# Weight blocks and activation planes placed modulo 256 bytes, and a down projection in three passes instead of two

## The reference, cut to what matters

```python
h = h + hybrid_mixer(rms_norm(h, g), w_in, ...)      # w_in 1024 x 3592, w_out 1024 x 1024
h = h + conv_ffn(rms_norm(h, g), w_up, ..., w_down)  # w_up 1024 x 5632, w_down 2816 x 1024
...
for l in range(2):
    h = h + 0.5 * swiglu(rmsnorm(h, ffn1_norm[l]), w_gate, w_up, w_down)   # 1024 x 2816 twice, 2816 x 1024
    h = h + hybrid_mixer_2(rmsnorm(h, mix_norm[l]), w_in, ...)             # 1024 x 4608 and three smaller
    h = h + 0.5 * swiglu(rmsnorm(h, ffn2_norm[l]), w_gate, w_up, w_down)
```

## Time and profile before

| | |
|---|---|
| median of three runs | 1459.07 us (1458.87 to 1459.16) |
| the profiled execution's own time | 1458.79 us |
| its span, first to last instruction | 1457.0 us |
| around the span | 1.8 us |
| TensorE matmuls, busy / share / count | 1449.5 us, 99%, 11473 |
| VectorE busy | 903.2 us, 62% |
| ScalarE busy | 770.0 us, 53% |
| GpSimd busy | 493.6 us, 34% |
| DMA, mean | 172 GB/s |

### The profile page before, as it was taken

The page is one execution under the profiler, slowest core; times in us unless marked ns, Lnnn a source line. Parts: engine busy times, 40 slices in busy tenths (PEclk is TensorE's granted clock), DMA queues, the critical chain, the costliest instruction groups (busy, mean ns, idle before and its releaser), DMA issues.

```text
span 1457.0 us, 30945 instructions
## 1 busy us (share of the span) xinstructions
PE 1449.5 (99%) x11473; PEld 1417.6 (97%) x11473; DVE 903.2 (62%) x1576; ACT 770.0 (53%) x1113; POOL 493.6 (34%) x213
## 2 busy tenths in 40 slices
PE   9999999999999999999999999999999999999998
PEld 8899999889999999999999999999999999999987
DVE  6438888756446469988644434444447898864533
ACT  6546555555444446567544544444444657654443
POOL 6550000534334303710333432433420570044342
PEclk9999999999999999999999999999999999999999
DMA  7435666645556445455555654655644635567763
GB/s 269 131 113 162 177 185 203 210 149 173 173 173 213 163 131 165 143 156 166 175 175 173 203 180 129 185 172 182 201 151 145 174 119 186 174 195 202 208 189 114
DMA packets 74634, 250.92 MB, mean 172 GB/s; under 512 B 15808, under 2 KB 16704, under 8 KB 74560
## 3 DMA queue, kind: packets, MB, share of 16 engines
q1 hardware_dynamic: 74272, 249.38, 55.5%
q10 hardware_dynamic: 288, 0.54, 0.1%
HBM read 247.79 MB, written 1.05 MB: 171 GB/s over the span
## 4 chain that ended last, share of the span: by engine, by line
PE 98%; DVE 1%; ACT 0%; issue 0%; DVEq 0%; ACTq 0%
PE W L1697 27%; PE W L1698 27%; PE W L1699 27%; PE W L1785 3%; PE XP L1849 2%; PE XQ L1849 2%; PE W L1784 1%; PE W L1749 1%; PE W L1800 1%; PE W L1799 1%; PE W L1750 1%; PE W L1798 1%; PE W L1751 1%; PE XQ L1962 0%; PE XP L1854 0%
## 5 line engine op out<-in xcount | busy, mean ns | idle before, releaser
L463 POOL TENSOR_TENSOR wlo<-raw,whi 128x1024 fp32r<-128x1024 f32 (+1 forms) x185 | 473.1, 2562 | 913.0 <-ACT whi L538 912.6
L1697 PE MATMUL W<-xh,whi 128*128 128x272 f32 (+2 forms) x2400 | 689.6, 287 | 0.0
L1698 PE MATMUL W<-xl,whi 128*128 128x272 f32 (+2 forms) x2400 | 687.5, 286 | 0.0
L1699 PE MATMUL W<-xh,wlo 128*128 128x272 f32 (+2 forms) x2400 | 685.8, 286 | 0.0
L538 ACT ACTIVATE whi<-raw 128x1024 fp32r<-128x1024 f32 (+1 forms) x440 | 480.6, 1098 | 109.7 <-PE W L1699 68.2
L1697 PEld LDWEIGHTS W<-xh,whi 128*128 128x128 f32 x2400 | 452.4, 189 | 2.2 <-issue 1.2
L1699 PEld LDWEIGHTS W<-xh,wlo 128*128 128x128 f32 x2400 | 452.3, 188 | 0.0
L1698 PEld LDWEIGHTS W<-xl,whi 128*128 128x128 f32 x2400 | 451.1, 188 | 0.2
L1023 DVE TENSOR_TENSOR wlo<-raw,whi 128x1024 fp32r<-128x1024 f32 (+1 forms) x255 | 331.8, 1302 | 80.3 <-ACT whi L538 80.0
L1697 PE MATMUL W<-ax,whi 128*128 128x272 f32 (+2 forms) x816 | 234.5, 287 | 0.4 <-DVE ax L1467 0.3
L1699 PE MATMUL W<-ax,wlo 128*128 128x272 f32 (+2 forms) x816 | 234.3, 287 | 0.0
(11 more groups left out here) (293 smaller groups left out, 1401.0 us busy)
## 6 DMA issues: line engine op xcount, KB each, us to landing
raw<-in_w SPq DMA_DIRECT2D x377, 512.0 KB, 3.7
raw<-in_w SPq DMA_DIRECT2D x64, 704.0 KB, 4.1
proj<-proj SPq DMA_DIRECT2D x16, 64.0 KB, 3.8
scr<-in_cst SPq DMA_DIRECT2D x1, 1000.0 KB, 8.3
h<-in_hT SPq DMA_DIRECT2D x3, 272.0 KB, 4.4
raw<-in_w SPq DMA_DIRECT2D x2, 256.0 KB, 3.8
proj<-in_gain SPq DMA_DIRECT2D x1, 512.0 KB, 5.0
out<-proj SPq DMA_DIRECT2D x4, 128.0 KB, 1.8
```

Source lines behind the costliest of these rows:

```text
L463: pool.tensor_tensor(wlo[:, j, 0:cols], raw[:, j, 0:cols], whi[:, j, 0:cols].bitcast(F32), ALU.subtract).then_inc(lo_ready[j], 1)
L1697: pe.matmul(out, whi[:, j, w], mh, start=start and k == 0, stop=False, skip_group_check=True)
L1698: pe.matmul(out, whi[:, j, w], ml, start=False, stop=False, skip_group_check=True)
L1699: ins = pe.matmul(out, wlo[:, j, w], mh, start=False, stop=stop and k == len(rhs) - 1, skip_group_check=True)
```

## The change

Four things change together.

1. **Weight blocks** are written to `whi` and `wlo` not back to back but at a place and with a step that follow the moving operand: `step` is 128 + 16 against `xh` and `xl` (whose chunks step by 272), 128 + 32 against `ax` in the products over 1024 channels, 128 in the down projections. The place is worked out so that a weight block always begins 16 elements (64 bytes) past the beginning of its moving chunk modulo 64 (26 elements where the first token is 14). Slots are 1440 wide instead of 1408. `raw` stays packed. In the last down projection the moving weights begin where the stationary activation begins modulo 64.
2. **`ax`** becomes `[P, 2, FC, ROW]` with ROW = 288, so `ah` and `al` of a chunk begin at the same place modulo 64 and chunks alternate between two places. The chunks of a down projection are dealt to its two slabs by parity (0, 2, 4... and 1, 3, 5...), so that inside a slab the place is constant.
3. **The first down projection** uses the three passes of `slab`, 256 columns each; `halves` and `residual_halves` are gone, and `residual` makes one addition where two were.
4. **Room**: `cst` keeps 256 columns, its other 688 land in a part of `proj` by a second DMA, and VectorE waits for GpSimd's copy of them (`minus_ready`) before it writes to that part. GpSimd's loops over slabs of the first projections and of the mixers are written out.

```diff
+LINE, PITCH = 64, S11 + 32
+WHI_AT, WLO_AT, X_AT, ROW = 0, 0, 0, T + 16
+Place = namedtuple("Place", "blocks width step hi lo")
+X_BEHIND = {0: -16, T_A: -26, T_B: -16}
+ACT_BEHIND = {0: (-16, -16), T_A: (-26, -26), T_B: (-16, -16)}
+DOWN_BEHIND = {0: (-16, -16), T_B: (-16, -16)}
+TOKEN_BEHIND = (0, 0)
+def column(moving, weights, j, behind):
+    return (moving - weights - LINE // 2 * (j % 2) - behind) % LINE
+def x_place(t, j):
+    return Place(DC, P, P + T % LINE, column(X_AT + t, WHI_AT, j, X_BEHIND[t]), column(X_AT + t, WLO_AT, j, X_BEHIND[t]))
...
+def d_places(t):
+    high, low = DOWN_BEHIND[t]
+    return tuple(Place(HALF, P, P, column(X_AT + t + j % 2 * ROW, WHI_AT, j, high),
+                       column(X_AT + t + j % 2 * ROW, WLO_AT, j, low)) for j in range(4))
...
-        whi = sb("whi", [P, 4, S11], F32R)
-        wlo = sb("wlo", [P, 4, S11], F32R)
+        whi = sb("whi", [P, 4, PITCH], F32R)
+        wlo = sb("wlo", [P, 4, PITCH], F32R)
...
-        ax = sb("ax", [P, FC, 2, T], F32R)
-        ah, al = ax[:, :, 0, :], ax[:, :, 1, :]
+        ax = sb("ax", [P, 2, FC, ROW], F32R)
+        ah, al = ax[:, 0, :, 0:T], ax[:, 1, :, 0:T]
...
+        def spread(weights, at, j, place, a=0, e=None):
+            e = place.blocks if e is None else e
+            return weights[:, j, at + place.step * a:at + place.step * e].rearrange(
+                "p (k n) -> p k n", n=place.step)[:, :, 0:place.width]
...
-            sp.dma_start(cst[:, :], cst_d).then_inc(cst_landed, 16)
+            sp.dma_start(cst[:, :], cst_d[:, 0:2 * P]).then_inc(cst_landed, 16)
+            sp.dma_start(signs, cst_d[:, 2 * P:]).then_inc(cst_landed, 16)
...
-                act.activation(whi[:, j, 0:cols], raw[:, j, 0:cols], ACT.Copy).then_inc(hi_ready[j], 1)
+                act.activation(high(j, place), packed(j, place), ACT.Copy).then_inc(hi_ready[j], 1)
...
-                    dve.tensor_tensor(wlo[:, slot, 0:cols], raw[:, slot, 0:cols], whi[:, slot, 0:cols].bitcast(F32),
+                    dve.tensor_tensor(low(slot, place), packed(slot, place), high(slot, place).bitcast(F32),
                                       ALU.subtract).then_inc(lo_ready[slot], 1)
...
-                        if j % 2 and t == T_B:
-                            residual_halves(2 * i + j // 2, j - 1, 4 * (g + i) + j + 1, coef, 0)
-                        elif j % 2:
+                        if j % 2:
                             residual(p, 2 * i + j // 2, j - 1, 4 * (g + i) + j + 1, 2, coef, t)
...
+                    if s == RG:
+                        dve.wait_ge(minus_ready, 1)
...
-                        if t == T_B:
-                            halves(g + i, j, f, half, j - half, first and j < 2).then_inc(mm_done, 1)
-                            continue
-                        slab(g + i, j, a_rhs(t)[half * HALF:(half + 1) * HALF], W[j - half][:, t:T], start=half == 0,
-                             stop=half == 1, each=(al_ready, FC * f + half * HALF, 0) if first and j < 2 else None).then_inc(mm_done, 1)
+                        slab(g + i, j, d_rhs(t, half), W[j - half][:, t:T], start=half == 0, stop=half == 1,
+                             each=(al_ready, FC * f + half, 2) if first and j < 2 else None).then_inc(mm_done, 1)
...
 def down_slabs(w):
-    return [tiles(w[half * HALF * P:(half + 1) * HALF * P], c) for c in chunk_cols(0, DC) for half in range(2)]
+    rows = w.reshape(FC, P, D)
+    return [tiles(rows[half::2].reshape(HALF * P, D), c) for c in chunk_cols(0, DC) for half in range(2)]
```

More of the change, by code:

```diff
@@ L21 @@
+from collections import namedtuple
 from contextlib import ExitStack
@@ L537, in hi @@
                     act.wait_ge(mm_done, 4 * g + j - 3)
-                act.activation(whi[:, j, 0:cols], raw[:, j, 0:cols], ACT.Copy).then_inc(hi_ready[j], 1)
+                act.activation(high(j, place), packed(j, place), ACT.Copy).then_inc(hi_ready[j], 1)
             def hi_ahead(g, j, own, nxt):
-                dg, slot, cols, _ = ahead(j, own, nxt)
-                hi(g + dg, slot, cols, first=isinstance(g, int) and g + dg == 0)
+                dg, slot, place, _ = ahead(j, own, nxt)
+                hi(g + dg, slot, place, first=isinstance(g, int) and g + dg == 0)
             def sqrt_stat(p, t=0, fin=False):
@@ L705, in _ @@
             hi_part(1, 1)
-            hi(0, 2, S8, first=True)
+            hi(0, 2, first_x(2)[2], first=True)
             act.wait_ge(mm_done, 1)
@@ L1688, in emptied, with slab, act_pairs, a_rhs @@
                     pe.wait_ge(evac_done, n)
-            def slab(g, j, rhs, out, at=0, start=True, stop=True, each=None, between=None):
+            def slab(g, j, rhs, out, at=0, start=True, stop=True, each=None):
+                places, pairs = rhs
                 pe.wait_ge(lo_ready[j], g + 1)
-                for k, (mh, ml) in enumerate(rhs):
-                    if each is not None and k >= each[2]:
-                        pe.wait_ge(each[0], each[1] + k - each[2] + 1)
-                    w = slice((at + k) * P, (at + k + 1) * P)
-                    pe.matmul(out, whi[:, j, w], mh, start=start and k == 0, stop=False, skip_group_check=True)
-                    pe.matmul(out, whi[:, j, w], ml, start=False, stop=False, skip_group_check=True)
-                    ins = pe.matmul(out, wlo[:, j, w], mh, start=False, stop=stop and k == len(rhs) - 1,
+                for k, (mh, ml) in enumerate(pairs):
+                    if each is not None:
+                        pe.wait_ge(each[0], each[1] + each[2] * k + 1)
+                    wh, wl = weights(j, places[j], at + k)
+                    pe.matmul(out, wh, mh, start=start and k == 0, stop=False, skip_group_check=True)
+                    pe.matmul(out, wh, ml, start=False, stop=False, skip_group_check=True)
+                    ins = pe.matmul(out, wl, mh, start=False, stop=stop and k == len(pairs) - 1,
                                     skip_group_check=True)
-                    if between is not None and k < len(rhs) - 1:
-                        between(k)
                 return ins
             def x_rhs(t=0):
-                return [(xh[:, k, t:], xl[:, k, t:]) for k in range(DC)]
-            def a_rhs(t=0):
-                return [(ah[:, k, t:], al[:, k, t:]) for k in range(FC)]
+                return x_places(t), [(xh[:, k, t:], xl[:, k, t:]) for k in range(DC)]
+            def act_pairs(t, chunks):
+                return [(ah[:, c, t:], al[:, c, t:]) for c in chunks]
+            def a_rhs(t, *chunks):
+                return a_places(t), act_pairs(t, chunks)
+            def d_rhs(t, half):
+                return d_places(t), act_pairs(t, range(half, FC, 2))
             X_RHS = x_rhs()
@@ L1728, in stat, with project @@
                 pe.matmul(X[3][:, t:T], ones, acc[:, t:], start=True, stop=True, skip_group_check=True).then_inc(stat_mm, 1)
-            def project(g, j, rhs, each=None, behind=3, t=0, between=None):
+            def project(g, j, rhs, behind=3, t=0):
                 emptied(4 * g + j - behind)
-                slab(g, j, rhs, W[j][:, t:T], each=each, between=between).then_inc(mm_done, 1)
+                slab(g, j, rhs, W[j][:, t:T]).then_inc(mm_done, 1)
             STAT_AT = 5
@@ L1773, in ffn_up @@
                         project(g + i, j, x_rhs(t), t=t)
-            def halves(g, j, f, half, out, first):
-                pe.wait_ge(lo_ready[j], g + 1)
-                both = W[out][:, :].rearrange("p (s n) -> p s n", s=2)
-                for k in range(HALF):
-                    c = half * HALF + k
-                    if first:
-                        pe.wait_ge(al_ready, FC * f + c + 1)
-                    w = slice(k * P, (k + 1) * P)
-                    pe.matmul(W[out][:, 0:T - T_B], wlo[:, j, w], ah[:, c, T_B:], start=c == 0, stop=False, skip_group_check=True)
-                    ins = pe.matmul(both, whi[:, j, w], ax[:, c, :, T_B:], start=False, stop=c == FC - 1, skip_group_check=True)
-                return ins
             def last_down(g, f):
@@ L2188, in mixer @@
                 for s in range(2, 4 * N_MIX):
-                    ts = t if s >= G_QK or (s >= G_V and s % 2 == 0) else 0
+                    ts = mixer_token(s, t)
                     project(g + s // 4, s % 4, x_rhs(ts), t=ts)
```

311 lines of the change are left out of this document (174 added, 137 removed).

## The result

The changed kernel takes **1447.45 us** (median of four runs, 1447.29 to 1448.09) against 1459.01 us of the kernel before on the same chip: 11.6 us less, a ratio of 0.9922 (95% interval 0.9909 to 0.9934). The forecast was 1422.0, 36 us less. So the sign and the range hold, and the size is a third of the 36.3 us that I gave; it lies where the shallow case stood. The profiled execution's own time is 1447.49 us, its span 1445.7 us.

A forecast was written before the change was run, and what follows sets the result against it. TensorE's time between matmul starts was taken as the bound. Gains of 26.2 + 10.1 (placement), 0.9 (three passes) and 0.4 (last addition) less 1.3 (VectorE) made 36.3 us off 1458.8, so 1422 us; range 1393 to 1451.

The forecast's parts named there:

- the shallow case: Rival: crossing to the next block, or half the passes, still collides; a quarter to half the gain, 1441 to 1450; chance 0.17.
- What bounds the kernel: TensorE, busy 99% of the span; an edit is worth what it takes from time between matmul starts or few stops.
- The relation of the two addresses: Inference that how weight and moving reads stand to each other sets 3 to 5 ns of a pass.
- The "no effect" rival: Surplus belongs to a pass and its weight load whatever the addresses; 1460 us, chance 0.08.
- The term "placement": Counted matmul passes: 272 columns from 126.1 to 122.0 ns, 256 from 118.3 to 115.0; 26.2 and 10.1 us gained.
- The 16 columns: Ten better-placed passes of 256 columns plus 16 columns at 2.4 GHz (6.7 ns) give 121.7 ns for 272.
- Three passes: First down projection: 350 to 345 ns a block, 0.9 us gained with placement; alone it costs 0.9 us.
- The split with gaps: Weight writes in eight stepped pieces cost ScalarE some 17 ns, others as little; free while three slabs of cover hold.
- VectorE in the mixers: Middle of both mixers: VectorE 94% busy, its waits no longer all fit; half of 2.6 us lost, 1.3.
- The deeper case: Rival: nothing collides any more; 256 columns at 114 ns, 272 at 120.7; 1409, down to 1395; chance 0.17.
- The slower case: Rival: a fixed relation can be bad, every pass 4 ns longer; 38 us more, 1497; chance 0.06.
- the change doesn't do what it says: Rival: tiles begin elsewhere modulo 256 bytes, so the relation is constant but another; about 1455, chance 0.02.

The follow-up runs named there:

- The runs with TensorE alone: Kernels without the whole computation, only weight loads and matmuls over zeros at varied address distances; 272 columns took 123.8 ns at 12 ahead, 127.0 at 8.
- The kernel that sits at 60 ahead: Changed kernel with distances slow with TensorE alone, from xh and xl only: 60 ahead at 272 columns, 4 at 258, 52 at 256; 1453.38 us.
- the last one: Second tuned version (distances chosen per width and for alternating slabs) with 12 ahead instead of 16 at 272 columns from xh and xl; 1440.92 us, ratio 0.9874.

## Why the prediction was right in kind and wrong in size

**What bounds the kernel: right.** The stops of TensorE are as before (the longest 1.2 us, no new one over 0.4 us), and all of the gain is in the time between starts.

**The relation of the two addresses: right as a cause, but not the only one, and not of the whole surplus.** I had called it an inference that the relation makes the interval vary. The runs with TensorE alone show it: 123.8 ns at 12 ahead and 127.0 at 8 ahead from every entry, and in the kernel the packed blocks bring 126.1 back. The "no effect" rival is gone. What I didn't have is the second cause, what stood before. And I wrote of the 12.8 ns over the columns' 113.3 that this is what the change reaches for: at the best distance of any run, 122.7, 9.4 of them remain, and what they are stays open. The Trainium skill (SBUF — State Buffer, Who interferes with whom) lets the moving operand and the weight loads read through two independent ports. By that alone the distance of their addresses would change nothing; here it changes a pass of 272 columns by 3.2 ns and one of 512, 0 ahead against 4 ahead, by 4.8, so the measurement decides against taking the rule as far as this.

**The term "placement": the step that failed.** I took 122.0 ns for 272 columns and 115.0 for 256, from short stretches of six and ten passes, "what ordinary passes hold for a while". They measured 124.3 and 123.5 ns (from `xh`, and in the down projections), 117.5 and 116.0. The term of 26.2 us was 7.6 + 3.2 = 10.8 us, the small groups with it, and that of 10.1 us was 1.3 - 0.5 = 0.8 us from `xh` and next to nothing from `ax`. Together they are 11.6 us where I had 36.3; the other terms were small and nearly cancel, so this is nearly the whole miss. A short stretch shows what a pass can do after some others, not what a fixed distance sustains: with TensorE alone most distances lie at 125 to 127 ns, where the kernel was already. Over the sixteen distances in slabs the mean is 125.2, so a constant distance drawn at random is worth 0.9 ns over the changing ones' 126.1, and I had priced it by the best moments of the changing ones at 4.1. That 16 ahead was among the good ones for 272 columns is luck; nothing in the rows before pointed to it.

**The 16 columns.** I scaled the ten passes of 256 columns up to 272 by the columns alone and leaned on it. The two widths have different good distances (in slabs 12 or 16 ahead against 42 or 22, from one entry for the latter), so a figure of one says little for the other. The same goes for 258 columns and for the last down projection: the first became 0.6 ns slower and the second 3.9 ns, and I had given the one a gain and the other nothing.

**Three passes: right in sign, half the size.** Forecast 0.9 us, from 350 to 345 ns a block. Within a slab a pass takes 114.2 ns, but the ends of the slabs cost more, and the mean over the projection is 116.0: 348 ns a block, 61.2 us for 61.6. Of the last addition's 0.4 us nothing can be told apart; the additions are the x16 row below for the x8 of the earlier trace rows, 422 ns each as before.

**The split with gaps, the order of the chunks, the constants: free, as forecast.** VectorE, ScalarE and GpSimd, groups by line and shape of the changed kernel:

```profile
L1111 DVE TENSOR_TENSOR wlo<-raw,whi 128x1024 fp32r<-128x1024 f32 x223 | 278.4, 1249 | 59.4 <-ACT whi L618 59.0
...
L1146 DVE SCALAR_TENSOR_TENSOR h<-W,h 128x256 f32<-128x256 f32 x16 | 6.7, 422 | 17.2 <-PE W L1786 16.3 <-PE W L1843 0.8
```

```profile
L618 ACT ACTIVATE whi<-raw 128x1024 fp32r<-128x1024 f32 x376 | 393.3, 1052 | 90.5 <-PE W L1786 51.6 <-PE W L1879 16.8 <-PE XP L1879 9.2
```

```profile
L538 POOL TENSOR_TENSOR wlo<-raw,whi 128x1024 fp32r<-128x1024 f32 x153 | 369.4, 2421 | 633.9 <-ACT whi L618 633.4 <-DVE scr L1387 0.4
```

Packed they took 1250, 1052 and 2407 ns. The pieces cost VectorE and ScalarE nothing and GpSimd 14 ns of 2421, less than the 17 ns I took from the earlier trace rows. TensorE doesn't wait for any of them more than before, and all that isn't one of the listed kinds of pass, the start with the two DMAs of constants among it, grew by 0.2 us.

**VectorE in the mixers: not seen.** It is busy 49.0 of 52.0 us and 40.5 of 43.0, 94% as in the earlier trace rows. Taking together the passes from `xh` and `xl` there that last over 25 ns longer than the median, their surplus over it is 1.2 us where it was 1.3, so no new waits came. Since TensorE became only 1.5% faster here, the condition of this term hardly arose; whether 1.3 us would be right for the full gain stays open. The 2.6 us of which it is half were a little high too: the 329 passes of 272 columns and 264 of 256 in the two stretches give 2.2 us by my own intervals.

**The rivals.** The shallow case, 1441 to 1450, held the result by luck, for another reason than the one I gave. I had the crossing between blocks or half of the passes colliding; but the down projections, which have no such crossing, gain no more, 125.6 to 123.5 ns. The deeper case had no ground, and the range's lower end, 1393, doesn't follow from it either: its own sum ends at 1395. The slower case was right that a fixed relation can be bad, in parts: 258 columns and the last down projection lost. That the change doesn't do what it says is out, since 16 ahead takes 124.2 ns alone and 124.3 in the kernel. The Trainium skill (TensorE: Matmul & The Clock Gate, Back-to-back issue gap) has a formula, N/2.4 + 2.5 ns, that leaves weight loads out; my estimate from it is 115.8 ns for 272 columns and 109.2 for 256. The best that any run with weight loads held was 122.7 and 113.1, so the measurement stays 4 to 7 ns above that estimate at every place.

What stays open is why certain distances collide. The runs have the interval as a function of the distance, the width and the entry, and nothing in them shows how the memory is divided, or whether 64 elements is the whole period.

## What to carry to other kernels

If TensorE is busy throughout and the interval of its passes is longer than their columns, run the passes alone over all distances of the two addresses, with the kernel's own widths and slab shapes, before the layout is changed. Choose a distance that gives the same interval from several entries, choose it for each width, and change alternating slabs together. Price a fixed state by what is sustained, over 50 passes and more, and never by six.

## What was not expected of the hardware

- The same instructions at the same addresses settle in one of two intervals and hold it for 96 passes, 122.8 or 125.0 ns at 48 ahead and 123.8 or 127.2 at 60, by what stands ahead of them. The kernel that sits at 60 ahead varied more over its four runs (1450.55 to 1455.02 us, against 1440.47 to 1441.43 for the last one); that the one comes from the other isn't shown.
- The distance that is good for 272 columns is not that for 258 or 256, and for 512 moving columns an equal place of both operands is the worst in the layout of the last down projection (234.8 ns for 230.0).
- Writing eight pieces of 128 elements with gaps costs VectorE and ScalarE no more than one piece (1249 and 1052 ns for 1250 and 1052), and GpSimd 14 ns of 2421.
